# Last step of five feed-forwards: 512-column matmuls and sums of halves in place of three 256-column matmuls per block

## The chip, the core and the metric

The kernel runs on one core of one Trainium2 chip. The time is device time in microseconds of one execution. TensorE multiplies (its weight loads are listed apart, as PEld), VectorE (DVE), ScalarE (ACT) and GpSimd (POOL) do the rest, and SyncE (SP) issues the loads of the weights.

## The reference

Two transformer blocks over 256 tokens of width 1024, batch 1, in fp32. What matters here are its five feed-forward phases: a mixture of 32 experts of width 128, computed for all tokens and combined with routing weights, and four SwiGLU feed-forwards of width 2816 = 22 x 128.

```python
for e in range(N_EXPERTS):                                   # 32 experts
    hid = jax.nn.silu(xf @ w_gate[e]) * (xf @ w_up[e])
    y = y + combine[:, e:e + 1] * (hid @ w_down[e])

def swiglu(x, w_gate, w_up, w_down):                         # four times, D_FF = 2816
    return (jax.nn.silu(x @ w_gate) * (x @ w_up)) @ w_down
```

Between them stand a gated linear attention and a sparse attention (before the experts), a recurrent block (between `ffn0` and `ffn1`), keys and values (before `ffn2`) and an attention (before `ffn3`). Each of the four SwiGLU results is normalised (RMS) and added to the residual, half of it; the result of the experts is added directly.

## The kernel before

Every product is computed from operands split in two: `hi`, the value rounded to the matmul's fp32r format, and `lo`, the remainder. A product a*b is a_hi*b_hi + a_hi*b_lo + a_lo*b_hi, summed in PSUM; the helper `mm3` issues these three matmuls (lines 661 to 663).

Weights come in pieces of 128 x 1024 through a ring of six slots. SyncE loads a piece into `raw`, ScalarE rounds it to `w_hi` (line 1527, in loops line 1592), VectorE subtracts to get `w_lo` (line 2046, in loops 2051), and TensorE uses it. The order on each engine is written out by hand, and semaphores join them: `raw_in`, `hi_done`, `lo_done`, `used`.

A feed-forward of n steps (n = 32 for the experts, phase `moe`; n = 22 for `ffn0` to `ffn3`) handles 128 hidden channels per step f: the gate product, the up product, and the down product of step f - 1, one piece each. The hidden values are channel by token, 128 x 256. Two ways exist for a gate or up product of eight blocks of 128 inputs:

- `channel_major`, narrow: `mm3` for each block, 24 matmuls of 256 columns into one half of a PSUM bank.
- `channel_major_wide`: `both` holds the activations' `hi` and `lo` side by side, so one matmul of 512 columns gives w_hi*x_hi in the left half of the bank and w_hi*x_lo in the right one; w_lo*x_hi, 256 columns, is added to the left half. That is 8 matmuls of 512 and 8 of 256 columns (lines 747, 749, 750), and VectorE has to add the two halves (`tensor_reduce`, lines 2113 and 2153).

The steps inside a feed-forward are wide. The last step, n - 1, is narrow in the kernel before, in all five phases.

What VectorE does in a step: `scale_gate` multiplies the gate product by `rb`, the norm's factor per token (narrow: line 2110 straight from PSUM; wide: sum of halves, line 2113, then the multiply, line 2116). ScalarE applies SiLU (line 1587). `hidden` multiplies by `rb` again (line 2140), in `moe` by the combine weight (line 2145), then by the up product (narrow: line 2150; wide: sum of halves, line 2153, then line 2156), rounds it to `hid_hi` (line 2161) and takes the remainder `hid_lo` (line 2163), which releases TensorE's down product.

In the last step ScalarE splits the next phase's pieces behind SiLU, and `hidden` is given `beside`, the `w_lo` of the next piece, which VectorE does between line 2140 and the up product. `ffn3` is the last phase and has none. TensorE, behind its last up product, does the six matmuls of the down product of step n - 2 for the first token tile and first two column halves, waits for the last step's `hid_lo` (`hid_ready`), and then issues 18 more. The first finished quarter of the result goes to VectorE's residual sum (line 2257, in `moe`) or ScalarE's squares (line 1652).

Of the kernel before, what the change touches and what calls it, by code (L numbers as in the profile page):

```python
# [159 lines left out]
HID0 = {"moe": 0, "ffn0": E_N, "ffn1": E_N + FT, "ffn2": E_N + 2 * FT, "ffn3": E_N + 3 * FT}  # L160
# [8 lines left out]
def two_blocks(nc, A, consts, out):  # L169
    with ExitStack() as ctx:  # L170
# [78 lines left out]
        def sig(name):  # L249
            if name not in names:  # L250
                names[name] = sem(name)
            return names[name]
# [405 lines left out]
        def _(pe):  # L658
# [75 lines left out]
            def channel_major(s, o, step, xT=(xT_hi, xT_lo)):  # L734

                hi, lo = slot_view(w_hi, s, KT, P), slot_view(w_lo, s, KT, P)
                for k in range(KT):
                    m = mm3(o, hi[:, k, :], lo[:, k, :], xT[0][:, k, :], xT[1][:, k, :], k == 0, k == KT - 1)
                m.then_inc(used, step)
# [37 lines left out]
            def feed_forward(ph, n, begin, between, after_second=None, both=xT_both, norm_n=None):  # L777
                b = PLAN.start[ph]
                c0 = HID0[ph]
# [10 lines left out]
                def up_narrow(i, par, step):  # L790
                    s = (b + 3 * par) % RING
                    xT = (both[:, 0], both[:, 1])
                    pe.wait_ge(lo_done, i + 1)
                    channel_major(s, ps[:, 4 + par, 0:T], 1, xT)
                    pe.wait_ge(lo_done, i + 2)
                    channel_major((s + 1) % RING, ps[:, 6 + par, 0:T], step, xT)
# [8 lines left out]
                def down(hc, i, par, first, last, s=None):  # L805

                    if s is None:
                        s = (b + 3 * (1 - par) + 2) % RING
                    pe.wait_ge(hid_ready, hc)
                    pe.wait_ge(lo_done, i + 1)  # L810
                    for t in range(NT):
                        for h in range(2):
                            m = down_part(s, par, t, h, first, last)
                    m.then_inc(used, 1)
# [32 lines left out]
                f = n - 2  # L847
                up(None, f * 3 + b, 0)
                down(f + c0, f * 3 + b + 2, 1, False, False)
                up_narrow(f * 3 + b + 3, 1, 1)  # L850


                s0, s1 = (b + 3 * n - 1) % RING, (b + 3 * n) % RING
# [513 lines left out]
            b = PLAN.start["kv"]  # L1367
# [664 lines left out]
        def _(dve):  # L2032
# [7 lines left out]
            def lo(i, cols=PIECE, parts=P):  # L2040

                if i >= len(PLAN.real) or not PLAN.real[i]:
                    return
                dve.wait_ge(hi_done, i + 1)
                s = i % RING
                dve.tensor_tensor(w_lo[0:parts, s, 0:cols], raw[0:parts, s, 0:cols], w_hi[0:parts, s, 0:cols].bitcast(F32),  # L2046
                                  ALU.subtract).then_inc(lo_done, PLAN.step(i))

            def lo_at(s, w):
                dve.wait_ge(hi_done, w)  # L2050
                dve.tensor_tensor(w_lo[:, s, :], raw[:, s, :], w_hi[:, s, :].bitcast(F32), ALU.subtract)\  # L2051
                    .then_inc(lo_done, 1)
# [53 lines left out]
            def scale_gate(w_used, par, bank, both=None):  # L2106

                if both is None:
                    dve.wait_ge(used, w_used)
                    dve.tensor_tensor(sil[:, par, :], ps[:, bank, 0:T], rb[:], ALU.mult).then_inc(gate_scaled, 1)  # L2110
                    return
                dve.wait_ge(used, w_used)
                dve.tensor_reduce(sil[:, par, :], ps[:, bank, :].rearrange("p (a t) -> p t a", a=2), AX_X, ALU.add)\  # L2113
                    .then_inc(gate_sum, 1)
                dve.wait_ge(gate_sum, both)
                dve.tensor_tensor(sil[:, par, :], sil[:, par, :], rb[:], ALU.mult).then_inc(gate_scaled, 1)  # L2116

            def unweighted(f, w_used, bank):


                dve.wait_ge(silu_done, f + 1)
                dve.tensor_tensor(sil[:, f, :], sil[:, f, :], rb[:], ALU.mult).then_inc(hid_scl, 1)
                dve.wait_ge(hid_scl, f + 1)
                dve.wait_ge(used, w_used)
                dve.tensor_tensor(hid[:, f, :], sil[:, f, :], ps[:, bank, 0:T], ALU.mult).then_inc(hid_mul, 1)
# [40 lines left out]
            def feed_forward(ph, n, norm_n):  # L2166
                b, c0, moe = PLAN.start[ph], HID0[ph], ph == "moe"

                w0 = c0 - 2 * list(HID0).index(ph) - 3

                def step(f, pieces, beside=None):
                    for i in pieces[:2]:
                        lo(i)
                    if f == 0:
                        dve.wait_ge(norm_rb, RB_AT[norm_n])
                    banks = (4 + f % 2, 6 + f % 2)
                    wide = w0 + f if (3 if moe else 0) < f < n - 1 else None
                    scale_gate(b + 3 * f + 1, f % 2, banks[0], wide)
                    for i in pieces[2:]:
                        lo(i)  # L2180
                    c = c0 + f + 1
                    hidden(c, b + 3 * f + 2, f % 2, f if moe else None, c, f + 1, banks[1], beside, wide)

                if moe:
                    dve.wait_ge(norm_rb, RB_AT[1])
                    scale_gate(b + 1, 0, 0)
                    scale_gate(b + 4, 1, 5)
                    lo(b + 7)
                    unweighted(0, b + 3, 1)
                    unweighted(1, b + 5, 7)  # L2190
                    lo(b + 8)
                    lo(b + 9)
                    dve.wait_ge(sig("comb01_ok"), 1)
                    weighted(0)
                    weighted(1)
                    lo(b + 10)
                    scale_gate(b + 6, 0, 4)
                    lo(b + 11)
                    dve.wait_ge(sig("comb2_in"), 16)
                    hidden(3, b + 7, 0, 2, 3, 3, 6, free=b + 10)  # L2200
                    lo(b + 12)
                    scale_gate(b + 8, 1, 5)
                    lo(b + 13)
                    hidden(4, b + 9, 1, 3, 4, 4, 7, free=b + 11)
                    lo(b + 14)
                    dve.wait_ge(sig("comb_in"), 32)
                elif LEAD[ph] == 3:
                    lo(b + 4)
                    lo(b + 5)
                    dve.wait_ge(norm_rb, RB_AT[norm_n])  # L2210
                    scale_gate(b + 1, 0, 0)
                    lo(b + 6)
                    hidden(c0 + 1, b + 3, 0, None, c0 + 1, None, 1)
                    scale_gate(b + 4, 1, 5, w0 + 1)
                    lo(b + 7)
                    hidden(c0 + 2, b + 5, 1, None, c0 + 2, None, 7, both=w0 + 1)
                    lo(b + 8)
                    scale_gate(b + 6, 0, 4, w0 + 2)
                    lo(b + 9)
                    lo(b + 10)  # L2220
                    hidden(c0 + 3, b + 7, 0, None, c0 + 3, None, 6, both=w0 + 2, free=b + 8)
                    lo(b + 11)
                    scale_gate(b + 10, 1, 5, w0 + 3)
                    lo(b + 12)
                    hidden(c0 + 4, b + 11, 1, None, c0 + 4, None, 7, both=w0 + 3, free=b + 9)
                    lo(b + 13)
                    lo(b + 14)
                else:
                    step(0, [b + 3, b + 4, b + 5])
                    step(1, [b + 6, b + 7, b + 8])  # L2230
                with dve.Fori(4 if LEAD[ph] > 1 else 2, n - 2, 2) as f:
                    i0 = dve.snap(f * 3 + b)
                    for par in range(2):
                        for j in range(3):
                            off = 3 * par + 3 + j
                            lo_at((b + off) % RING, i0 + (off + 1))
                            if j == 1:
                                scale_gate(i0 + (3 * par + 1), par, 4 + par, dve.snap(f + (w0 + par)))
                        c = dve.snap(f + (c0 + par + 1))
                        e = dve.snap(f + par) if moe else None  # L2240
                        hidden(c, i0 + (3 * par + 2), par, e, c, c, 6 + par, None, dve.snap(f + (w0 + par)))
                step(n - 2, [b + 3 * n - 3, b + 3 * n - 2, b + 3 * n - 1])
                step(n - 1, [b + 3 * n], lambda: lo(b + 3 * n + 1))
                lo(b + 3 * n + 2)
# [492 lines left out]
            b = PLAN.start["kv"]  # L2737
# [34 lines left out]
            b = PLAN.start["q"]  # L2772
# [89 lines left out]
```

## Time and profile before

| | |
|---|---|
| median of three runs | 1543.87 us (1543.37 to 1545.18) |
| profiled execution | 1542.71 us, span 1540.8 us |
| TensorE busy (matmuls) | 1497.6 us, 97% |
| VectorE busy | 1201.1 us, 78% |
| ScalarE busy | 790.4 us, 51% |
| narrow multiplies of a gate product (line 2110) | 13, median 420 ns |
| sums of halves (lines 2113 and 2153) | 107 each, medians 691 and 692 ns |
| multiplies behind them (lines 2116 and 2156) | 107 each, median 425 ns |

The busy times of the engines overlap. A matmul's listed duration contains its way through the array, so matmuls that follow one another overlap: what one costs in a row of them is the distance from start to start. In a timeline the bracket behind a row tells how long the engine was idle before it and which instruction ended that.

### The profile page before, as it was taken

The numbers are of one execution on the slowest core, as the hardware profiler recorded it, in microseconds if no ns is written. First come the engines' busy times: TensorE is split into PE (matmuls) and PEld (weight loads), VectorE is DVE, ScalarE is ACT, GpSimd is POOL, SyncE is SP. The second block draws the span as 40 slices with busy tenths as digits, with TensorE's granted clock in tenths as the row PEclk, the third lists the DMA queues.
The fourth block names the chain that finished last, engine by engine and source line by source line (L and its number), as shares of the span: only waits on it lengthen the run. The fifth ranks groups of instructions, "written<-read, shape, count | busy, mean of one in ns | idle before, by whom it ended". The sixth has DMA issues, their size and how long they took to land.

```text
span 1540.8 us, 23595 instructions
## 1 busy us (share of the span) xinstructions
PE 1497.6 (97%) x8186; PEld 1282.1 (83%) x8186; DVE 1201.1 (78%) x2164; ACT 790.4 (51%) x1196; POOL 43.5 (3%) x68
## 2 busy tenths in 40 slices
PE   7989999999999999999999999999999999999998
PEld 6767789888888888887878888888888889888886
DVE  4876477988888888778688878785887786598886
ACT  6548554444444544446796434465444465554443
POOL 4100000000000300000000000000000000000000
PEclk9999999999999999999999999999999999999999
DMA  9635445755555676655244766644766643356661
GB/s 258 176 106 186 137 137 198 272 186 198 191 179 164 188 217 189 192 176 180 60 124 153 220 188 190 191 141 148 216 193 190 185 145 110 101 180 203 197 189 57
DMA packets 258540, 266.20 MB, mean 173 GB/s; under 512 B 10512, under 2 KB 210496, under 8 KB 258224
## 3 DMA queue, kind: packets, MB, share of 16 engines
q1 hardware_dynamic: 255040, 255.87, 54.7%
q0 software_dynamic: 3440, 9.54, 2.3%
q8 instruction: 36, 0.59, 0.2%
q14 instruction: 24, 0.20, 0.0%
HBM read 264.21 MB, written 1.09 MB: 172 GB/s over the span
## 4 chain that ended last, share of the span: by engine, by line
PE 85%; DVE 9%; ACT 4%; issue 2%; DMA 0%; DVEq 0%; SPq 0%; ACTq 0%
PE ps L747 22%; PE ps L661 13%; PE ps L749 13%; PE ps L663 13%; PE ps L662 13%; PE ps L750 3%; DVE w_lo L2046 2%; DVE xT_both L2090 1%; PE ps L1255 1%; ACT w_hi L1527 1%; PE ps L1416 1%; ACT sq L1652 0%; PE ps L691 0%; ACT xT_both L1536 0%; DVE arena L2333 0%
## 5 line engine op out<-in xcount | busy, mean ns | idle before, releaser
L1592 ACT ACTIVATE w_hi<-raw 128x1024 fp32r<-128x1024 f32 x276 | 290.8, 1058 | 159.3 <-PE ps L663 138.6
L2051 DVE TENSOR_TENSOR w_lo<-raw,w_hi 128x1024 fp32r<-128x1024 f32 x276 | 328.8, 1219 | 1.0
L747 PE MATMUL ps<-xT_both,w_hi 128*128 128x512 f32 x1218 | 306.6, 391 | 0.0
L2046 DVE TENSOR_TENSOR w_lo<-raw,w_hi 128x1024 fp32r<-128x1024 f32 (+4 forms) x209 | 247.1, 1210 | 42.3 <-ACT w_hi L1527 40.4
L747 PEld LDWEIGHTS ps<-xT_both,w_hi 128*128 128x128 f32 x1218 | 228.9, 188 | 45.9
L1587 ACT ACTIVATE hid_sil<-hid_sil 128x256 f32<-128x256 f32 x120 | 50.1, 418 | 360.1 <-DVE hid_sil L2116 318.9
L1527 ACT ACTIVATE w_hi<-raw 128x1024 fp32r<-128x1024 f32 (+4 forms) x209 | 210.9, 1048 | 29.6 <-PE ps L663 25.8
L749 PEld LDWEIGHTS ps<-xT_both,w_lo 128*128 128x128 f32 x1392 | 189.9, 190 | 13.6
L749 PE MATMUL ps<-xT_both,w_lo 128*128 128x256 f32 x1392 | 194.1, 282 | 0.0
L661 PE MATMUL ps<-w_hi,hid_hi 128*128 128x512 f32 x480 | 188.5, 393 | 0.8 <-DVE hid_lo L2163 0.7
L663 PE MATMUL ps<-w_hi,hid_lo 128*128 128x512 f32 x480 | 187.3, 390 | 0.0
L662 PE MATMUL ps<-w_lo,hid_hi 128*128 128x512 f32 x480 | 186.8, 389 | 0.0
L661 PE MATMUL ps<-w_hi,xT_both 128*128 128x512 f32 (+3 forms) x360 | 141.9, 394 | 13.7 <-DVE w_lo L2046 12.3
L2113 DVE TENSOR_REDUCE hid_sil<-ps 128x256 f32<-128x512 f32 x107 | 73.8, 690 | 98.9 <-PE ps L750 98.9
L663 PE MATMUL ps<-w_hi,xT_both 128*128 128x512 f32 (+3 forms) x360 | 137.8, 383 | 0.0
L662 PE MATMUL ps<-w_lo,xT_both 128*128 128x512 f32 (+3 forms) x360 | 137.7, 382 | 0.0
L663 PEld LDWEIGHTS ps<-w_hi,hid_lo 128*128 128x128 f32 x480 | 90.1, 188 | 20.0
L662 PEld LDWEIGHTS ps<-w_lo,hid_hi 128*128 128x128 f32 x480 | 90.2, 188 | 19.1
L661 PEld LDWEIGHTS ps<-w_hi,hid_hi 128*128 128x128 f32 x480 | 90.5, 188 | 17.8 <-DVE hid_lo L2163 3.3
L661 PEld LDWEIGHTS ps<-w_hi,xT_both 128*128 128x128 f32 (+1 forms) x360 | 68.7, 191 | 30.9 <-DVE w_lo L2046 9.2
L2153 DVE TENSOR_REDUCE hid_sil<-ps 128x256 f32<-128x512 f32 x107 | 74.0, 691 | 17.8 <-PE ps L750 15.1
L663 PEld LDWEIGHTS ps<-w_hi,xT_both 128*128 128x128 f32 (+1 forms) x360 | 68.5, 190 | 12.8
(395 smaller groups left out, 2160.0 us busy)
## 6 DMA issues: line engine op xcount, KB each, us to landing
raw<-in_ffn_w_gate_dram SPq DMA_DIRECT2D x88, 512.0 KB, 4.2
raw<-in_ffn_w_up_dram SPq DMA_DIRECT2D x88, 512.0 KB, 5.3
raw<-in_ffn_w_down_dram SPq DMA_DIRECT2D x88, 512.0 KB, 4.1
raw<-in_w_in_dram SPq DMA_DIRECT2D x40, 512.0 KB, 4.9
raw<-in_w_gate_dram SPq DMA_DIRECT2D x32, 512.0 KB, 3.5
raw<-in_w_up_dram SPq DMA_DIRECT2D x32, 512.0 KB, 4.3
raw<-in_w_down_dram SPq DMA_DIRECT2D x32, 512.0 KB, 3.5
raw<-in_rg_w_in_dram SPq DMA_DIRECT2D x16, 512.0 KB, 4.7
```

The lines of the kernel that those rows point to most:

```text
L661: pe.matmul(o, a_hi, b_hi, start=start, stop=False)
L662: pe.matmul(o, a_hi, b_lo, start=False, stop=False)
L663: return pe.matmul(o, a_lo, b_hi, start=False, stop=stop)
L747: pe.matmul(o, hi[:, k, :], both[:, :, k, :], start=k == 0, stop=False)
L749: pe.matmul(ps[:, bank, 0:T], lo[:, k, :], both[:, 0, k, :], start=False, stop=False)
L1527: act.activation(w_hi[0:parts, i % RING, 0:cols], raw[0:parts, i % RING, 0:cols], ACT.Copy)\
L1587: act.activation(sil[:, par, :], sil[:, par, :], ACT.Silu).then_inc(silu_done, 1)
L1592: act.activation(w_hi[:, s, :], raw[:, s, :], ACT.Copy).then_inc(hi_done, 1)
L2046: dve.tensor_tensor(w_lo[0:parts, s, 0:cols], raw[0:parts, s, 0:cols], w_hi[0:parts, s, 0:cols].bitcast(F32), ALU.subtract).then_inc(lo_do ...
L2051: dve.tensor_tensor(w_lo[:, s, :], raw[:, s, :], w_hi[:, s, :].bitcast(F32), ALU.subtract)\
L2113: dve.tensor_reduce(sil[:, par, :], ps[:, bank, :].rearrange("p (a t) -> p t a", a=2), AX_X, ALU.add)\
L2153: dve.tensor_reduce(hid[:, par, :], ps[:, bank, :].rearrange("p (a t) -> p t a", a=2), AX_X, ALU.add)\
```

## The change

TensorE's last step calls `up`, which is wide, in place of `up_narrow`. On VectorE the condition for `wide` includes the last step, and the count of sums done before a phase (`w0`) takes one less off per earlier phase, since each now has one step more with sums. Nothing else changes: the pieces, the loads, the order on ScalarE, GpSimd and SyncE are the same.

```diff
@@ TensorE, feed_forward
                 up(None, f * 3 + b, 0)
                 down(f + c0, f * 3 + b + 2, 1, False, False)
-                up_narrow(f * 3 + b + 3, 1, 1)
+                up(None, f * 3 + b + 3, 1)
@@ VectorE, feed_forward
-                w0 = c0 - 2 * list(HID0).index(ph) - 3
+                w0 = c0 - list(HID0).index(ph) - 3
...
                     banks = (4 + f % 2, 6 + f % 2)
-                    wide = w0 + f if (3 if moe else 0) < f < n - 1 else None
+                    wide = w0 + f if (3 if moe else 0) < f else None
                     scale_gate(b + 3 * f + 1, f % 2, banks[0], wide)
```

On TensorE, the start of the last step of `ffn0` stands like this before: behind the down product the three matmuls of `mm3` for the first block of the gate product, 256 columns each, which come eight times for the gate and eight times for the up product.

```order
L661 MATMUL ps<-w_hi,hid_hi 128x512
L662 MATMUL ps<-w_lo,hid_hi 128x512
L663 MATMUL ps<-w_hi,hid_lo 128x512
L661 MATMUL ps<-xT_both,w_hi 128x256
L662 MATMUL ps<-xT_both,w_hi 128x256
L663 MATMUL ps<-xT_both,w_lo 128x256
```

Now the same place, up to the next down product:

```order
L663 MATMUL ps<-w_hi,hid_lo 128x512
L747 MATMUL ps<-xT_both,w_hi 128x512 x7
L749 MATMUL ps<-xT_both,w_lo 128x256 x8
L750 MATMUL ps<-xT_both,w_hi 128x512
L747 MATMUL ps<-xT_both,w_hi 128x512 x7
L749 MATMUL ps<-xT_both,w_lo 128x256 x8
L750 MATMUL ps<-xT_both,w_hi 128x512
L661 MATMUL ps<-w_hi,hid_hi 128x512
```

48 matmuls have become 32, the first 16 for the gate and the last 16 for the up product; what stands ahead and behind is the same.

On VectorE, the last step of `ffn0` before, from the split of one piece to the remainder that TensorE waits for:

```order
L2046 TENSOR_TENSOR w_lo<-raw,w_hi 128x1024
L2110 TENSOR_TENSOR hid_sil<-ps,rb 128x256
L2140 TENSOR_TENSOR hid_sil<-hid_sil,rb 128x256
L2046 TENSOR_TENSOR w_lo<-raw,w_hi 128x1024
L2150 TENSOR_TENSOR hid_sil<-hid_sil,ps 128x256
L2161 CAST hid_hi<-hid_sil 128x256
L2163 TENSOR_TENSOR hid_lo<-hid_sil,hid_hi 128x256
```

And now:

```order
L2046 TENSOR_TENSOR w_lo<-raw,w_hi 128x1024
L2113 TENSOR_REDUCE hid_sil<-ps 128x256
L2116 TENSOR_TENSOR hid_sil<-hid_sil,rb 128x256
L2140 TENSOR_TENSOR hid_sil<-hid_sil,rb 128x256
L2046 TENSOR_TENSOR w_lo<-raw,w_hi 128x1024
L2153 TENSOR_REDUCE hid_sil<-ps 128x256
L2156 TENSOR_TENSOR hid_sil<-hid_sil 128x256
L2161 CAST hid_hi<-hid_sil 128x256
L2163 TENSOR_TENSOR hid_lo<-hid_sil,hid_hi 128x256
```

Each read of a product from PSUM has become a sum and a multiply; the split of a piece stands between the two products as before. The other four ends change alike, with the combine weight's multiply (line 2145) behind the split in `moe`, and without that split in `ffn3`.

## Rows read from the trace of the kernel before

**Rows 1.** The page: busy time by engine, and the last chain by engine.
```profile
PE 1497.6 (97%) x8186; PEld 1282.1 (83%) x8186; DVE 1201.1 (78%) x2164; ACT 790.4 (51%) x1196; POOL 43.5 (3%) x68
PE 85%; DVE 9%; ACT 4%; issue 2%; DMA 0%; DVEq 0%; SPq 0%; ACTq 0%
```

**Rows 2.** TensorE's waits: us in total, times, longest us.
```profile
PE ps L661 <- DVE hid_lo L2163: 0.7, 2, 0.5
```

**Rows 3.** Timeline, ffn3's step before the last: start us, us, engine, line, operation.
```profile
1513.20 1.75 PE L747 MATMUL ps<-xT_both,w_hi 128*128 128x512 f32 x7
...
1515.98 1.77 PE L747 MATMUL ps<-xT_both,w_hi 128*128 128x512 f32 x7
1516.18 0.69 DVE L2113 TENSOR_REDUCE hid_sil<-ps 128x256 f32<-128x512 f32 x1 [1.24 <-PE ps L750]
...
1517.36 0.42 ACT L1587 ACTIVATE hid_sil<-hid_sil 128x256 f32<-128x256 f32 x1 [2.84 <-DVE hid_sil L2116]
...
1518.77 0.40 PE L661 MATMUL ps<-w_hi,hid_hi 128*128 128x512 f32 x1
...
1519.04 0.69 DVE L2153 TENSOR_REDUCE hid_sil<-ps 128x256 f32<-128x512 f32 x1 [0.24 <-PE ps L750]
...
1520.22 0.29 DVE L2161 CAST hid_hi<-hid_sil 128x256 fp32r<-128x256 f32 x1
```

**Rows 4.** Timeline, ffn3's last step and what follows it.
```profile
1521.51 0.28 PE L661 MATMUL ps<-xT_both,w_hi 128*128 128x256 f32 x1
...
1524.58 0.42 DVE L2110 TENSOR_TENSOR hid_sil<-ps,rb 128x256 f32<-128x256 f32 x1 [2.47 <-PE ps L663]
...
1525.04 0.42 ACT L1587 ACTIVATE hid_sil<-hid_sil 128x256 f32<-128x256 f32 x1 [6.31 <-DVE hid_sil L2110]
...
1527.26 0.40 PE L661 MATMUL ps<-w_hi,hid_hi 128*128 128x512 f32 x1
...
1527.53 0.42 DVE L2150 TENSOR_TENSOR hid_sil<-hid_sil,ps 128x256 f32<-128x256 f32 x1 [1.61 <-PE ps L663]
...
1527.99 0.29 DVE L2161 CAST hid_hi<-hid_sil 128x256 fp32r<-128x256 f32 x1
...
1528.80 0.50 PE L661 MATMUL ps<-w_hi,hid_hi 128*128 128x512 f32 x1
...
1529.80 0.60 ACT L1652 ACTIVATE sq<-ps 128x512 f32<-128x512 f32 x1 [2.82 <-PE ps L663]
```

**Rows 5.** Timeline, the end of ffn1's last step.
```profile
1006.39 0.42 DVE L2110 TENSOR_TENSOR hid_sil<-ps,rb 128x256 f32<-128x256 f32 x1 [2.47 <-PE ps L663]
...
1007.17 2.94 ACT L1527 ACTIVATE w_hi<-raw 128x1024 fp32r<-128x1024 f32 x3
...
1008.25 1.22 DVE L2046 TENSOR_TENSOR w_lo<-raw,w_hi 128x1024 fp32r<-128x1024 f32 x1 [0.52 <-ACT w_hi L1527]
...
1009.39 0.41 DVE L2150 TENSOR_TENSOR hid_sil<-hid_sil,ps 128x256 f32<-128x256 f32 x1
...
1010.23 0.39 PE L663 MATMUL ps<-w_hi,hid_lo 128*128 128x512 f32 x1
...
1010.65 0.50 PE L661 MATMUL ps<-w_hi,hid_hi 128*128 128x512 f32 x1
...
1011.64 0.60 ACT L1652 ACTIVATE sq<-ps 128x512 f32<-128x512 f32 x1
```

**Rows 6.** Timeline, the end of the last step of moe.
```profile
498.87 0.42 DVE L2145 TENSOR_TENSOR hid_sil<-hid_sil,arena 128x256 f32<-128x256 f32 x1
...
500.59 0.50 PE L661 MATMUL ps<-w_hi,hid_hi 128*128 128x512 f32 x1 [0.49 <-DVE hid_lo L2163]
```

**Rows 7.** Stretches: us, busy by engine, PEclk (granted clock), DMA share, GB/s.
```profile
60.41:66.30 5.89, 3.41 (x15) 2.89 (x16) 5.79 (x9) 4.44 (x5) 0.00 (x0) 1.00 0.41 126
98.30:102.46 4.16, 0.00 (x0) 0.00 (x0) 4.09 (x6) 3.31 (x4) 0.00 (x0) 0.99 0.01 2
102.46:105.93 3.47, 3.47 (x9) 2.76 (x9) 3.44 (x3) 0.00 (x0) 0.00 (x0) 0.52 0.67 195
```

## The prediction

> **What bounds the kernel now.** I read the page's shares first: TensorE is busy 97% of the span, VectorE 78%, and the chain that ended last is TensorE for 85% and VectorE for 9% [rows 1]. So what counts is TensorE's own time and the few places where it waits. The waits view has only one entry in which TensorE waits for the hidden values of a feed-forward: 0.7 us in 2 waits [rows 2]. Read alone, this says that the last step's work on VectorE is nearly hidden. Whether it is hidden with room to spare only the timeline tells, so next I read the end of three feed-forwards.
>
> A wide step is seen in [rows 3] (step 20 of `ffn3`), the narrow last step behind it in [rows 4], the end of `ffn1` in [rows 5], which stands for `ffn0`, `ffn1` and `ffn2` (three ends with the same distances within 0.02 us), the end of `moe` in [rows 6]. In [rows 5] the six matmuls that cover the wait end at 1010.23 + 0.39 = 1010.62, and the next matmul, which needs `hid_lo`, starts at 1010.65. TensorE stands still for 0.03 us: the two engines arrive together. In `moe` it already waits, 0.49 us [rows 6]. There is no slack under VectorE's chain at any of these ends. The chain from the first half of the last step is: gate sum on VectorE, SiLU on ScalarE, scaling by `rb`, then the split of the next piece (`w_lo`), then the up product, the rounding, the remainder, and TensorE goes on.
>
> **TensorE's part.** The narrow step has 2 x 24 matmuls of 256 columns, the wide one 2 x (8 of 512 and 8 of 256): the same 12,288 columns, in 32 instructions in place of 48. The wide pair takes 1518.77 - 1513.20 = 5.57 us [rows 3], the narrow pair 1527.26 - 1521.51 = 5.75 us [rows 4]. Gain 0.18 us in each of five feed-forwards, 0.90 us in all if nothing waited. One wide half takes 2.78 (1513.20 to 1515.98).
>
> A rule speaks of this. By the Trainium skill, "TensorE: Matmul & The Clock Gate", section "Back-to-back issue gap", matmuls follow each other by their columns at 2.4 GHz and a fixed 2.5 ns. By it the narrow pair would take 5.24 us and the wide 5.20, an estimate, so the gain would be 0.04 us; the lead of 0.09 us that the sum below uses would be 0.02, four times, and the 0.18 of the last end 0.04, which makes the loss 0.42 us larger. The trace does not agree in this size (0.18), and I take the trace.
>
> **VectorE, first half (gate).** Narrow: one multiply, and SiLU starts 1525.04 - 1524.58 = 0.46 us after it [rows 4]. Wide: the sum of the halves, then the multiply, and SiLU starts 1517.36 - 1516.18 = 1.18 us after [rows 3]: +0.72. Against it the first half is ready earlier: the wide sum starts 1516.18 - 1513.20 = 2.98 us after the first matmul of the step, the narrow multiply 1524.58 - 1521.51 = 3.07. SiLU is therefore late by 0.72 - 0.09 = **0.63 us**.
>
> What is queued behind it: ScalarE splits the next pieces behind SiLU (`w_hi`, 1007.17), and VectorE's `w_lo` starts only when the first has come (1008.25, idle 0.52 until then) [rows 5]. So `w_lo` moves by the same 0.63 us, and the up product stands directly behind it at 1009.39, with no idle time. In `moe` the multiplication with the combine weights stands between (498.87) [rows 6]; it moves too.
>
> **VectorE, second half (up).** Narrow: product to rounding 1527.99 - 1527.53 = 0.46 us [rows 4]. Wide: sum, then product, to rounding 1520.22 - 1519.04 = 1.18 us [rows 3]: **+0.72 us**. It can't slip under anything, since VectorE runs in order and was held by `w_lo` until then. Nor does it wait for TensorE: in [rows 5] the wide pair would be ready about 1009.15 (1006.39 - 3.07 + 2.78 + (1519.04 - 1515.98)), and VectorE comes to it at 1009.39 + 0.63 = 1010.02.
>
> **Sum at `moe`, `ffn0`, `ffn1`, `ffn2`:** 0.63 + 0.72 = 1.35 us later, and the 0.18 us of TensorE turns into more waiting. TensorE's idle time goes from 0.49 to 0.49 + 0.18 + 1.35 = 2.02 us in `moe` and from 0.03 to 1.56 us in the other three. Four times 1.35 is 5.40 us.
>
> **Sum at `ffn3`.** It is the last phase and has no piece to split, so VectorE waits for TensorE before the up product (1.61 us idle, [rows 4]) and the late gate is covered by that idle time. TensorE brings the second half 0.18 us earlier, the sum of halves costs 0.72: **+0.54 us**.
>
> **What follows.** After TensorE resumes the same 18 matmuls run. The first ScalarE pass over the result starts 1011.64 - 1010.65 = 0.99 us after the resumption in `ffn1` [rows 5] and 1529.80 - 1528.80 = 1.00 us in `ffn3` [rows 4], where ScalarE is idle before it. So although in `ffn1` ScalarE comes to it straight from its table load, TensorE's result is just as late there; ScalarE is moved by 0.63 us only, TensorE by 1.35, and the whole 1.35 passes on. The later norm, its transposes and the next phase descend from this result.
>
> Total: 5.40 + 0.54 = 5.94 us. Nothing is added that the trace lacks; unknown is only what a longer stop of TensorE does (clock, below) and whether a later stage absorbs it. The lower bound is the loss wholly hidden or given back and the 0.90 us of TensorE kept, -0.9 us; the upper is four clock drops, +12.6 us. I take 5.94, since every link of it is a distance in the rows and the ends meet without slack. The profiled execution took 1542.71 us (span 1540.8 and 1.9 around it); with the change it would be 1548.65. The median of the runs is 1543.87, 1.16 us above that execution; with 5.94 it is 1549.81, **forecast 1549.8 us**, 0.38% slower.
>
> **Rivals.**
>
> *The next phase gives it back (not slower).* Place: the first pair of pieces behind each of the first four feed-forwards. If there the wait that ends last were one for pieces whose load or split is not moved, the 1.35 us would vanish in it; the 0.54 us of `ffn3`, behind which nothing comes, would stay, so +0.5 us, 1544.4 us. It decides where this phase stood for more than 1.35 us on something independent. For it: loads and ScalarE's splits move by 0.63 us at most. Against it: the chain is TensorE and VectorE for 94% and rows for a DMA are 0% [rows 1], and the residual and the norm can't start without the result. Were the gain of TensorE to come out as well, it would be 1543.0 us; for that the sums of halves would have to be covered, and the 0.03 us in [rows 5] leaves no cover. Chance 0.10, of which 0.01 for this last form.
>
> *TensorE's clock falls in the longer stops.* The trace shows a stretch with a stop of 5.89 - 3.41 = 2.48 us in which the granted clock stayed 1.00, that is 2.4 GHz, and one of 4.16 us after which it was 0.52 for 3.47 us, nearly all of it at 1.2 GHz [rows 7]. That costs 3.47 x 0.48 = 1.67 us each. Four times: +6.7 on top, 1556.5 us; only behind `moe`, whose stop is the longest: 1551.5 us. The stops I expect, 2.02 and 1.56 us, are shorter than the one that did no harm. The Trainium skill ("TensorE: Matmul & The Clock Gate", section "What's actually happening") says that the default is the slow clock and that activity releases it; the trace agrees, with 0.52 behind the long stop. Chance 0.05 for one or more.
>
> *Only one of the two terms is paid.* If the split of the next piece did not wait on ScalarE's order behind SiLU, the gate's delay would be hidden as in `ffn3`: 4 x 0.72 + 0.54 = 3.4 us, 1547.3 us. The 0.52 us of idle time before `w_lo`, released by ScalarE [rows 5], speaks against it. Chance 0.06.
>
> *The change doesn't do what it says* (the last step stays narrow somewhere): the order of the changed program shows all five ends wide on both engines. Chance nil.
>
> **How the numbers follow.** Forecast 0.79, given back 0.10, one term 0.06, clock 0.05. Its own range is 1548.3 to 1551.3: the terms are good to some 0.3 us together, the medians to about 1 us. For 8 in 10 with the neighbouring cases in part I take 1546.8 to 1552.5. A measurement of this kernel tells 0.2%, 3.1 us, from no change. Slower by more: the forecast, the clock and half of the one-term case, 0.87. Within: 0.12. Faster: 0.01, as even the pure gain of 0.90 us lies within.
>
> **What would show it.** In the changed profile: the waits view has TensorE waiting for `hid_lo` at all five ends, some 2.0, 1.6, 1.6, 1.6 and 0.7 us; SiLU at 1.18 us behind the gate's sum; `w_lo` moved with it; from the first matmul of the last step to the resumption 7.29 us in `ffn3` are now 7.83; granted clock 1.00 there. TensorE's busy time falls by some 0.9 us. If the stops are there but the span grows by less than 4 us, the giving back is right and the place is the next phase. If the resumption moves by 0.7 us only, the ScalarE link is wrong.

## The result and the profile after

The changed kernel took 1551.38 us (median of 5, 1549.63 to 1552.30) beside 1543.87 us for the kernel before (median of 5, 1542.76 to 1545.18): ratio 1.0047, 95% interval 1.0033 to 1.0062. It is slower by 7.5 us where 5.94 were forecast, within the range of 1546.8 to 1552.5 and 0.1 us above the narrower one that the prediction gives its own mechanism. Timed again it took 1550.27 beside 1544.43 us, ratio 1.0040 (1.0026 to 1.0054), 5.8 us. The profiled execution took 1549.63 us, with a span of 1547.8 us beside 1540.8.

The page of the changed kernel, busy time and last chain, answering to [rows 1]:

```profile
PE 1497.4 (97%) x8106; PEld 1277.7 (83%) x8106; DVE 1208.2 (78%) x2174; ACT 790.4 (51%) x1196; POOL 43.5 (3%) x68
PE 84%; DVE 10%; ACT 3%; issue 2%; DMA 0%; DVEq 0%; SPq 0%; ACTq 0%
```

There are 80 matmuls less, yet TensorE's busy time is 0.2 us less, not 0.9. The five ends alone have 0.87 us less; 0.53 us more than before stands ahead of the last step of `moe`, in code that the change does not touch, where the two executions also have their low clock in different places. VectorE has ten instructions and 7 us more. The page hardly shows the loss; TensorE's waits do (us in total, times, longest), answering to [rows 2]:

```profile
PE ps L661 <- DVE hid_lo L2163: 7.7, 6, 2.0
```

From 0.7 to 7.7 us, of which the five ends have 7.5. The end of `ffn3` in the timeline, answering to [rows 3, 4]:

```profile
1528.01 1.75 PE L747 MATMUL ps<-xT_both,w_hi 128*128 128x512 f32 x7
...
1530.98 0.69 DVE L2113 TENSOR_REDUCE hid_sil<-ps 128x256 f32<-128x512 f32 x1 [2.37 <-PE ps L750]
...
1532.16 0.42 ACT L1587 ACTIVATE hid_sil<-hid_sil 128x256 f32<-128x256 f32 x1 [6.94 <-DVE hid_sil L2116]
...
1533.57 0.40 PE L661 MATMUL ps<-w_hi,hid_hi 128*128 128x512 f32 x1
...
1533.84 0.69 DVE L2153 TENSOR_REDUCE hid_sil<-ps 128x256 f32<-128x512 f32 x1 [0.80 <-PE ps L750]
...
1535.03 0.29 DVE L2161 CAST hid_hi<-hid_sil 128x256 fp32r<-128x256 f32 x1
...
1535.83 0.50 PE L661 MATMUL ps<-w_hi,hid_hi 128*128 128x512 f32 x1 [0.72 <-DVE hid_lo L2163]
...
1536.83 0.60 ACT L1652 ACTIVATE sq<-ps 128x512 f32<-128x512 f32 x1 [2.74 <-PE ps L663]
```

TensorE's pair takes 1533.57 - 1528.01 = 5.56 us, the gate's sum starts 2.97 us after the first matmul, SiLU 1.18 after that, the rounding 1.19 after the second sum, and the resumption comes after 7.82 us (7.29 before). VectorE still waits 0.80 us for TensorE before the second sum (1.61 before): here the gate's delay is covered. The end of `ffn1`, answering to [rows 5]:

```profile
1006.99 1.75 PE L747 MATMUL ps<-xT_both,w_hi 128*128 128x512 f32 x7
...
1009.96 0.69 DVE L2113 TENSOR_REDUCE hid_sil<-ps 128x256 f32<-128x512 f32 x1 [2.37 <-PE ps L750]
...
1011.48 2.94 ACT L1527 ACTIVATE w_hi<-raw 128x1024 fp32r<-128x1024 f32 x3
...
1012.55 1.23 DVE L2046 TENSOR_TENSOR w_lo<-raw,w_hi 128x1024 fp32r<-128x1024 f32 x1 [0.52 <-ACT w_hi L1527]
...
1013.69 0.68 DVE L2153 TENSOR_REDUCE hid_sil<-ps 128x256 f32<-128x512 f32 x1
...
1015.68 0.50 PE L661 MATMUL ps<-w_hi,hid_hi 128*128 128x512 f32 x1 [1.58 <-DVE hid_lo L2163]
...
1016.67 0.60 ACT L1652 ACTIVATE sq<-ps 128x512 f32<-128x512 f32 x1 [0.75 <-PE ps L663]
```

`w_lo` starts 2.59 us behind the gate's first VectorE instruction (1.86 before), still with 0.52 us of waiting for ScalarE, and the second sum has no idle time ahead of it. TensorE stands still for 1.58 us where it stood for 0.03. The squares still start 0.99 us behind the resumption, and ScalarE now waits 0.75 us for them. The end of `moe`, answering to [rows 6]:

```profile
500.41 0.42 DVE L2145 TENSOR_TENSOR hid_sil<-hid_sil,arena 128x256 f32<-128x256 f32 x1
...
502.86 0.50 PE L661 MATMUL ps<-w_hi,hid_hi 128*128 128x512 f32 x1 [2.03 <-DVE hid_lo L2163]
```

The length of an end, from the last step's first matmul to the resumption, is the measure for all that follows. In the profiled executions:

| end | moe | ffn0 | ffn1 | ffn2 | ffn3 | sum of differences |
|---|---|---|---|---|---|---|
| before | 7.80 | 7.33 | 7.33 | 7.31 | 7.29 | |
| changed | 9.15 | 8.69 | 8.69 | 8.71 | 7.82 | +6.00 us |

Forecast was 5.94. The span grew by 7.0 us; nearly all of the rest, 0.92 us, is already there when the last step of `moe` begins (493.71 beside 492.79). Stretches of the changed kernel, columns as in [rows 7]:

```profile
62.48:65.90 3.42, 3.42 (x9) 2.73 (x10) 3.42 (x4) 1.82 (x2) 0.00 (x0) 0.55 0.78 230
502.86:506.30 3.44, 3.44 (x15) 2.87 (x16) 2.77 (x4) 0.00 (x0) 0.00 (x0) 1.00 0.64 174
```

The first stands behind the same early stop (2.43 us here) as the first of [rows 7]. There the granted clock stayed 1.00; here it is 0.55, mostly 1.2 GHz. This is code that the change does not touch. In the profiles of the other kernels below the beginning of that step lies 0.4 us earlier to 2.4 us later than before, and 0.4 earlier in one that has both products wide: the shift belongs to the execution, not to the change. Behind the new stop of `moe` the clock stayed 1.00 in this execution.

### The profile page after: what moved, and what is told of

Same layout as the page of the kernel before. It is cut to its first block, busy times and chain, and to the rows that moved or that the text cites. A ratio compares the mean times of both kernels' runs of the same rounds, so it can differ in the third digit from the quotient of the medians.

```text
span 1547.8 us, 23445 instructions
## 1 busy us (share of the span) xinstructions
PE 1497.4 (97%) x8106; PEld 1277.7 (83%) x8106; DVE 1208.2 (78%) x2174; ACT 790.4 (51%) x1196; POOL 43.5 (3%) x68
## 4 chain that ended last, share of the span: by engine, by line
PE 84%; DVE 10%; ACT 3%; issue 2%; DMA 0%; DVEq 0%; SPq 0%; ACTq 0%
PE ps L747 23%; PE ps L749 14%; PE ps L661 13%; PE ps L663 12%; PE ps L662 12%; PE ps L750 3%; DVE w_lo L2046 2%; DVE xT_both L2090 2%; PE ps L1255 1%; ACT w_hi L1527 1%; PE ps L1416 1%; PE ps L691 0%; ACT sq L1652 0%; ACT xT_both L1536 0%; DVE arena L2333 0%
## 5 line engine op out<-in xcount | busy, mean ns | idle before, releaser
L747 PE MATMUL ps<-xT_both,w_hi 128*128 128x512 f32 x1274 | 320.6, 391 | 0.0
L747 PEld LDWEIGHTS ps<-xT_both,w_hi 128*128 128x128 f32 x1274 | 239.4, 188 | 48.0
L749 PEld LDWEIGHTS ps<-xT_both,w_lo 128*128 128x128 f32 x1456 | 198.6, 190 | 14.2
L749 PE MATMUL ps<-xT_both,w_lo 128*128 128x256 f32 x1456 | 203.0, 282 | 0.0
L2113 DVE TENSOR_REDUCE hid_sil<-ps 128x256 f32<-128x512 f32 x112 | 77.3, 690 | 109.7 <-PE ps L750 109.6
L2153 DVE TENSOR_REDUCE hid_sil<-ps 128x256 f32<-128x512 f32 x112 | 77.4, 691 | 18.9 <-PE ps L750 16.2
```

Of the source, the lines that this page charges most:

```text
L747: pe.matmul(o, hi[:, k, :], both[:, :, k, :], start=k == 0, stop=False)
L749: pe.matmul(ps[:, bank, 0:T], lo[:, k, :], both[:, 0, k, :], start=False, stop=False)
L2153: dve.tensor_reduce(hid[:, par, :], ps[:, bank, :].rearrange("p (a t) -> p t a", a=2), AX_X, ALU.add)\
```

## The experiments

**The changed kernel again**, without an edit.

> The changed kernel unaltered, timed again. In its first profile the five ends add up to the 5.9 us of the forecast, but the span grew by 7.0 us; about 0.9 us of it was there before the last step of moe began. Theory (the first 0.9 us is spread between executions, not the change): the five ends again add 5.9 us in the profile (1.35 each at moe, ffn0, ffn1, ffn2 and 0.54 at ffn3), the shift at the beginning of the last step of moe is another number than 0.9, anywhere within 1 us of zero, and the median is 5 to 7 us over the kernel before. Rival (the longer program or its other layout costs 0.9 us or more ahead of the first changed instruction): that shift is 0.9 us again and the median is 7.5 us over.

1550.27 us (1549.86 to 1553.07), +5.8. The profile is that of the execution with 1553.07 us, span 1551.3. Its ends are 9.14, 8.69, 8.69, 8.71 and 7.83 us, +6.00 again. But the shift at the beginning of moe's last step was 1.57, not within 1 us of zero, and a new loss is seen behind the stop of `moe`. TensorE's timeline there (start us, us), and two stretches:

```profile
503.50 0.50 PE L661 MATMUL ps<-w_hi,hid_hi 128*128 128x512 f32 x1 [2.04 <-DVE hid_lo L2163]
...
504.71 0.63 PE L662 MATMUL ps<-w_lo,hid_hi 128*128 128x512 f32 x1
505.14 0.63 PE L663 MATMUL ps<-w_hi,hid_lo 128*128 128x512 f32 x1
...
509.34 2.17 PE L691 MATMUL ps<-con,x_res 128*128 128x128 f32 x16
...
513.25 0.39 PE L769 MATMUL ps<-xT_both,w_hi 128*128 128x256 f32 x1 [1.74 <-ACT xT_both L1536]
```

```profile
504.30:507.70 3.40, 3.40 (x9) 2.63 (x8) 1.61 (x3) 0.00 (x0) 0.00 (x0) 0.50 0.64 196
514.50:517.90 3.40, 3.40 (x18) 3.40 (x18) 3.20 (x12) 3.33 (x8) 3.10 (x6) 0.51 0.19 44
```

0.80 us behind the resumption the clock falls to 0.50 for 3.4 us, and matmuls follow each other by 0.43 us instead of 0.23. From the resumption to the transposes it takes 5.84 us, where the profile before it had 4.21: 1.6 us lost. A second fall stands in the norm behind `moe`, where TensorE waits 1.74 us (1.73 in the kernel before); together they cost 2.9 us by the starts of ffn0's last step, 1.2 of it in the norm. So the clock rival of the prediction is real at `moe`, in some executions. The fall in the norm is another matter: the wait there is as long without the change. Of the twelve profiles here, of all kernels, in which nothing fills it, seven have a fall, among them the two with one product wide and the one with the split moved, whose clock stayed behind the stop of `moe`.

**VectorE's part alone, and TensorE's part alone.** Both take one half of the change:

```diff
 VectorE's part alone: the changed kernel with
-                up(None, f * 3 + b + 3, 1)
+                up_narrow(f * 3 + b + 3, 1, 1)
 TensorE's part alone: the kernel before with
-                up_narrow(f * 3 + b + 3, 1, 1)
+                up(None, f * 3 + b + 3, 1)
```

> VectorE's part alone: TensorE's last step stays narrow (48 matmuls), VectorE sums both halves of the bank in it. The right half then holds what the step before left there, so the last step's values are not those of the reference; the work is that of the change. Theory (VectorE's and ScalarE's chain sets every end): SiLU comes 0.72 us later behind the gate product, the up part takes 0.72 us more; from the first matmul of the last step to the resumption 7.33 becomes 8.77 us in ffn0, ffn1 and ffn2, 7.80 becomes 9.24 in moe, 7.29 becomes 8.01 in ffn3: 4 x 1.44 + 0.72 = +6.5 us over the kernel before, 0.5 us more than the whole change. Rival (TensorE hides part of it): less than +5 us. Rival (wide matmuls are what costs): about zero here.

> TensorE's part alone: its last step is wide (32 matmuls), VectorE reads only the left half of the bank in it, so w_hi times the activations' remainder is left out of the last step. Theory: the gate product is ready 0.09 us earlier and the chain behind it moves by that, -0.09 us at moe, ffn0, ffn1 and ffn2; at ffn3, where TensorE comes last, -0.18 us: -0.5 us in all, less than can be timed. TensorE waits 0.09 us more at the first four ends. Rival (the 0.18 us comes out everywhere): -0.9 us and no longer waits. Rival (something in the wide step itself is slow): a positive difference.

Neither computes the last step's values in full: the first adds to each product what a wide step had left in the right half of the bank (the same bank is used by every second step), the second leaves out w_hi times the activations' remainder.

VectorE's part: 1551.89 us, ratio 1.0046 (1.0032 to 1.0060); ends 9.25, 8.79, 8.78, 8.77, 8.02: +6.56, expected 6.5. TensorE's part: 1543.61 us, ratio 0.9996 (0.9987 to 1.0005), no difference that the timing tells; ends 7.68, 7.23, 7.23, 7.26, 7.11: -0.55, expected -0.5. Its wait in `moe` is 0.58 us (0.49 before), as expected 0.09 more. All of the loss is VectorE's, and TensorE's 0.18 us comes out whole only at `ffn3`.

**One product wide, the other narrow.** In the last step only; an excerpt, for the gate wide. With the up product wide the two conditions change places, and the calls in the other steps take the counts that go with them:

```diff
-                up(None, f * 3 + b + 3, 1)
+                wide_narrow(f * 3 + b + 3, 1)    # or narrow_wide: channel_major_wide for one, channel_major for the other
-                    wide = w0 + f if (3 if moe else 0) < f else None
+                    wide_g = w0 + f if (3 if moe else 0) < f else None            # gate wide
+                    wide_u = w1 + f if (3 if moe else 0) < f < n - 1 else None    # up narrow
```

> In the last step only the gate product is wide (its sum of halves on VectorE), the up product narrow. Theory (ScalarE's order behind SiLU carries the gate's delay to w_lo and so to the up product): 0.63 us later at moe, ffn0, ffn1 and ffn2, and at ffn3, where VectorE has idle time before the up product, the delay is covered and TensorE's earlier end gives -0.09 us: +2.4 us in all. From the first matmul of the last step to the resumption 7.33 becomes 7.96 us in ffn1. Rival (only the up half is paid, the gate is hidden everywhere): 7.33 becomes 7.24 or stays, 0 us in all.

> In the last step only the up product is wide, the gate narrow. Theory: +0.72 us at moe, ffn0, ffn1 and ffn2, and 0.72 - 0.09 = +0.63 at ffn3: +3.5 us in all; from the first matmul of the last step to the resumption 7.33 becomes 8.05 us in ffn1. With the run of the wide gate alone this adds up to the whole change, 2.4 + 3.5 = 5.9. Rival (the two halves cover each other): the sum of the two runs differs from the whole change's by more than 0.5 us in the profiled distances.

Gate wide: 1546.24 beside 1543.88 us, ratio 1.0014 (1.0004 to 1.0024); ends 8.42, 7.96, 7.95, 7.99, 7.19, +2.45. Up wide: 1547.21 us, ratio 1.0022 (1.0013 to 1.0032); ends 8.52, 8.06, 8.06, 8.04, 7.93, +3.55. The two add up to 6.00, the whole change. Both terms of the prediction stand, and so does the cover of the gate at `ffn3`.

**`w_lo` behind `hid_lo`.** The split of the next piece leaves the chain:

```diff
-                step(n - 1, [b + 3 * n], lambda: lo(b + 3 * n + 1))
+                step(n - 1, [b + 3 * n])
+                lo(b + 3 * n + 1)
```

> The changed kernel with the split of the next piece on VectorE (w_lo) moved behind the remainder hid_lo in the last step. Theory (the gate's delay costs only because w_lo waits for ScalarE and stands ahead of the up product): all ends look like ffn3's, TensorE brings the up product last: from the first matmul of the last step to the resumption 7.83 us in ffn0 to ffn3 and the same in moe, where the kernel before had 7.80. So at the resumption +0.03 us in moe and about +0.5 at the other four. Behind it VectorE now has one split more (1.14 us) with only 0.71 us of idle time, so up to 0.4 us is lost there per end: +2 to +4 us over the kernel before, 2 to 4 us less than the whole change. Rival (the loss is in the sums alone, wherever w_lo stands): no gain against the whole change.

> Gate product wide, up product narrow, w_lo behind hid_lo: the one form in which TensorE's gain of the gate half is kept and the sum of halves is covered by the wait for the up product. Theory: from the first matmul of the last step to the resumption 7.29 - 0.09 = 7.20 us at all five ends, against 7.80, 7.33 (three) and 7.29 before: -0.6 in moe and -0.1 at each of the others, -1.0 us in all before what the moved split costs behind it (up to 0.4 us at three ends, and the residual sum of moe starts later, but its last part is set by TensorE). Between -1 and +0.5 us: no difference that can be timed, the profile has to show it. Rival (the split behind hid_lo delays the norm in full, 1.14 us at each): +3.5 us.

With both products wide: 1545.97 us, ratio 1.0013 (1.0003 to 1.0022), 4.3 and 5.4 us less than the changed kernel in its two timings. All five ends are alike: 7.82, 7.83, 7.83, 7.87, 7.83, in sum 3.9 us less than in the changed kernel. TensorE's waits for `hid_lo` (us in total, times, longest):

```profile
PE ps L661 <- DVE hid_lo L2163: 3.9, 6, 0.7
```

Five stops of 0.72 to 0.74 us in place of 2.03, three of 1.58, and 0.72: the gate's sum costs nothing once `w_lo` does not carry it to the up product. The 3.9 us are more than the gate's 2.45, since the split's own time has left the chain too. The kernel before with the split moved was not run, so what the move alone is worth is not shown. It cost less behind the ends than the 0.4 us per norm that I allowed: TensorE waits 0.58 us for the first `x_res` tile in `ffn1`, 0.50 before.

With the gate wide and the up product narrow the ends are the shortest of all, 7.19, 7.18, 7.19, 7.15, 7.19: -1.16 us. The time is 1544.72 beside 1543.88, ratio 1.0009 (0.9999 to 1.0018), no gain. VectorE behind the end of `ffn1`:

```profile
1010.30 0.42 DVE L2157 TENSOR_TENSOR hid_sil<-hid_sil,ps 128x256 f32<-128x256 f32 x1 [0.89 <-PE ps L663]
...
1011.43 2.35 DVE L2053 TENSOR_TENSOR w_lo<-raw,w_hi 128x1024 fp32r<-128x1024 f32 x2
1013.99 0.69 DVE L2279 TENSOR_TENSOR xn<-ps,g_post 128x512 f32<-128x512 f32 x1 [0.21 <-ACT sq L1659]
```

and TensorE's wait behind it:

```profile
1017.95 1.16 PE L691 MATMUL ps<-con,x_res 128*128 128x128 f32 x8 [1.14 <-DVE x_res L2297]
```

The end is 0.14 us shorter, but VectorE has two splits (2.35 us) ahead of the norm, ScalarE three and its table load behind a later SiLU, and TensorE then waits 1.14 us for `x_res` where it waited 0.50. Of the expectation (-1.0, up to 0.4 back at three ends) the first part came and the second was too small: 0.65 to 0.70 us went back at each of three. Only `moe` (-0.61) and `ffn3` (-0.10) keep their gain; a kernel with that form in these two alone would save 0.7 us, an estimate from these two ends, below what the timing tells, and was not run.

**More sums.** The up product's sum done again, with the same result:

```diff
                     dve.wait_ge(used, w_used)
+                    for _ in range(more):      # 1, or 4, in the last step
+                        link(dve.tensor_reduce(hid[:, par, :], ps[:, bank, :].rearrange("p (a t) -> p t a", a=2), AX_X, ALU.add))
```

> The changed kernel with the sum of halves of the up product done twice in the last step (same result). Theory (nothing covers VectorE's chain, 1 us there is 1 us of time): 0.72 us more at each of five ends, +3.6 us over the changed kernel; TensorE's waits become 2.75 us in moe, 2.3 at three ends and 1.44 in ffn3; the granted clock stays 1.00 behind them. Rival (a part is covered downstream): less than +2.5 us in the distances from end to end.

> The changed kernel with the sum of halves of the up product done five times in the last step (same result). Theory: 2.9 us more at each of five ends, +14.4 us over the changed kernel from the chain alone. TensorE now stops for 4.9 us in moe, 4.5 at three ends and 3.6 in ffn3, as long as the one stop of 4.16 us in the kernel before behind which its granted clock was 0.52; if the clock falls behind these too, each costs up to 1.7 us more: +14.4 to +22.8 us, I expect it at moe and at least one more, about +18. Rival (the clock rival of the prediction would also be right at 2 us): a lower clock already shows in the run with one more sum.

One more: 1556.99 beside 1543.83 us, ratio 1.0077 (1.0060 to 1.0094), 13.2 us. The ends are 9.87, 9.41, 9.41, 9.44, 8.55: +3.62 over the changed kernel, the term as expected. But the clock did not stay 1.00. TensorE's resumption in `moe` and the stretch around it:

```profile
503.66 0.79 PE L661 MATMUL ps<-w_hi,hid_hi 128*128 128x512 f32 x1 [2.76 <-DVE hid_lo L2166]
```

```profile
503.30:507.00 3.70, 3.34 (x8) 2.67 (x9) 2.50 (x4) 0.00 (x0) 0.00 (x0) 0.54 0.47 128
```

In this execution it fell at all of the first four ends, whose stops are 2.76 and three of 2.30 us, and in the norm behind `moe`. Behind `moe` a fall cost 1.5 us again, but from the resumption to the next end's last step the distances of `ffn0`, `ffn1` and `ffn2` grew by 0.8, 0.5 and 0.5 us only: at `ffn0` 1.6 us were lost up to the beginning of the norm, and half of it came back in the norm, where TensorE's wait of 0.5 us for `x_res` is gone. The four executions have mean clocks of 0.990 to 0.995 and times of 1553.1 to 1558.3 us. Four more: 1571.13 us, ratio 1.0172 (1.0155 to 1.0189), 27.3 us over before, of which the ends have 20.5. The stops of 4.9, 4.5 (three) and 3.6 us all had a fall of the clock with them, for 6.8 us at each but `moe`; at `ffn0`:

```profile
699.67:706.50 6.83, 6.83 (x18) 5.34 (x19) 4.68 (x11) 2.95 (x9) 0.00 (x0) 0.55 0.27 77
```

So 1 us on VectorE's chain is 1 us of time, and above it the clock adds more with a longer stop: from the resumption of `ffn0` to the last step of `ffn1` 2.1 us here, 0.8 with one more sum. The rival is right in this: the lower clock shows with one more sum, and in one of two profiles with none.

**The stops filled.** Matmuls that nobody reads, before the wait for the last `hid_lo`, and for two runs also in the norm behind `moe`, the only one ahead of a feed-forward that has none:

```diff
+                keep_warm({"moe": 14, "ffn3": 4}.get(ph, 10), 4)    # last run: moe 4, ffn3 1, others 3
                 pe.wait_ge(hid_ready, c0 + n)
-            WARM = {..., 2: (0, 0, 0), ...}
+            WARM = {..., 2: (0, 0, 12), ...}                        # last run: (0, 0, 3)
```

> The changed kernel, and TensorE's stop before hid_lo filled with matmuls whose result nobody reads (14 of 256 columns in moe, 10 in ffn0 to ffn2, 4 in ffn3, into a bank that is free). They end before hid_lo comes, so the ends keep their lengths (9.15, 8.69, 8.69, 8.70, 7.82 us from the last step's first matmul to the resumption). In one of two profiles of the changed kernel the granted clock fell to 1.2 GHz for 3.4 us right behind the stop of moe, in the other not. Theory (the part of the time above the forecast comes from such falls in some executions): no fall behind any of the five stops; the fall in the norm behind moe stays possible; median 5.4 to 6.6 us over the kernel before. Rival (the excess is elsewhere): 7 us or more.

> As the run with the filled stop, and twelve matmuls whose result nobody reads in the 1.74 us that TensorE waits in the norm behind moe, the one norm that has none in the kernel before. Theory: no fall of the granted clock between the first 120 us and the end in any execution; mean clock 0.996 or 0.997 in each; median 5 to 6 us over the kernel before (which has such a fall itself in some executions), 0.3 to 1 us below the run with the filled stop alone, and a narrower spread. Rival (the fall in the norm does not depend on that wait): clock and spread as with the filled stop alone.

Both missed, by my own arithmetic: 1561.67 us (ratio 1.0115, 1.0098 to 1.0132) and 1564.11 us (1.0131, 1.0114 to 1.0148). I had counted 0.12 us for each of them, the distance of the fp32r matmuls. They are fp32, and each is two matmuls in the trace; 14 of them take 5.85 us, not 1.7, and the end of `moe` becomes 12.80 us:

```profile
500.69 6.20 PE L671 MATMUL ps<-con 128*128 128x256 f32 x28
506.54 0.58 PE L661 MATMUL ps<-w_hi,hid_hi 128*128 128x512 f32 x1
```

Their times say nothing on the excess. In both profiles the clock did not fall behind any end or in that norm.

> The filled stops again, at the right size. In the two runs before, each call of 256 columns was two matmuls in the trace and took 0.44 us, so that the filling outlasted the stop by 3.7 us in moe. Now 4 calls in moe (1.8 us of the 2.03), 3 in ffn0 to ffn2 (1.3 of 1.57), 1 in ffn3 (0.4 of 0.72), 3 in the norm behind moe (1.3 of 1.74). Theory (what the changed kernel loses above 5.9 us is the granted clock's fall behind the stop of moe and in the norm behind it, in some executions): the ends keep 9.15, 8.69, 8.69, 8.70 and 7.82 us, the granted clock does not fall between 120 us and the end, and the five executions have no mean clock below 0.995; median 1549.0 to 1550.2 us, +5 to +6 over a before of about 1544. Rival (the excess is no matter of the clock): 1551 us or more, as in the first timing, with the ends unchanged.

1549.04 us (six executions, 1548.10 to 1549.32) beside 1543.81 us, ratio 1.0033 (1.0021 to 1.0045): +5.2 us. The ends are unchanged, 9.14, 8.68, 8.69, 8.71, 7.82. The end of `moe` and the 20 us around it:

```profile
499.81 1.89 PE L671 MATMUL ps<-con 128*128 128x256 f32 x8
502.01 0.50 PE L661 MATMUL ps<-w_hi,hid_hi 128*128 128x512 f32 x1 [0.31 <-DVE hid_lo L2164]
```

```profile
500.00:520.00 20.00, 19.26 (x119) 16.70 (x119) 15.69 (x41) 13.38 (x32) 12.37 (x13) 1.00 0.53 146
```

All six executions have a mean clock of 0.996 or 0.997. The ten executions of the unfilled changed kernel have 0.994 to 0.996 and reach from 1549.63 to 1553.07 us; the three of them with 0.996 took 1549.63, 1549.86 and 1550.27. The rival (1551 us or more) is out: with the stops and the norm filled, which changes no end, no execution is as long as the shortest of those ten. The run does not tell the two apart: a kernel with only the stops filled to measure was not run, and the wait in the norm stays unfilled in the kernel before. That 5.2 us is less than the 6.0 of the ends may come from executions of the kernel before that carry the norm's 1.2 us, where these do not; the interval (3.2 to 6.9 us) holds both, and it is not shown.

## Why the prediction was right, and where it was not

- *VectorE and ScalarE set the ends, without slack.* Right. The waits are 2.03, three of 1.57 or 1.58, and 0.72 us, where 2.02, 1.56 and 0.7 were forecast.
- *Gate +0.63, carried by ScalarE's order to `w_lo`.* Right: +0.62 to +0.68 with the gate alone wide, -0.10 at `ffn3`, and gone when `w_lo` stands behind.
- *Up +0.72.* Right: +0.72 or +0.73 at four ends, +0.64 at `ffn3`, as the terms say.
- *TensorE's gain of 0.18 us per pair.* Right: half of it, the gate's 0.09, moves the chain and is in the 0.63; the rest only lengthens four of the five stops. The 0.04 us that follows from the Trainium skill's formula ("TensorE: Matmul & The Clock Gate", section "Back-to-back issue gap") did not come: the part alone brought 0.18 at `ffn3`. That section gives the formula for a matmul by itself and says that a stream with weight loads goes by other distances, which the prediction passed over; the distances here are 0.12 us at 256 columns and 0.23 at 512.
- *All of it passes on.* Right: between the ends nothing is given back. The next end's start moves by the same amount, within 0.05 us, wherever the clock is alike.
- *The clock stays.* Wrong as a certainty: I reasoned from one stop of 2.48 us behind which the clock stayed and gave a fall 0.05. The same early stop had a fall in the changed kernel's first profile, and a stop of 2.04 us in the second. One quiet execution said too little. The rival's price of 1.67 us per fall was about right behind `moe` (1.6) and too high at `ffn0` to `ffn2` (0.8 and 0.5 with one more sum), and the norm behind `moe` was missing from it.
- *The size.* The sum of the ends is 6.0 us in both profiles of the changed kernel; the two timings gave 7.5 and 5.8, and both intervals (5.1 to 9.6 and 4.0 to 8.3 us) hold the forecast of 5.94. So the 1.5 us of the first timing above the ends are not clear of noise. Falls of the clock are what the profiles show that can make them, but how often the clock falls in the kernel before, where the early stop and the norm are the same, stays open: its executions also reach down to a mean clock of 0.994, and none of those was profiled.

## What to carry to other kernels

At the end of a loop count the chain that the last matmul releases, not the matmuls: there the sum that a wider matmul leaves to VectorE is paid in full, while inside the loop the next step's products cover it. Look then at what stands in order between the halves of such a chain; here moving one split of the next phase's weights out of it took back 3.9 of the 6.0 us. And one execution's granted clock is one draw: behind a new TensorE stop of 2 us one of two executions of the same program lost another 1.6 us.

## What the hardware showed that was not expected

- With stops of nearly the same length the granted clock fell in one execution and not in another. The early stop of 2.4 to 2.5 us, the same code in every kernel, had a fall in 7 of the 14 profiles (2.43 us in the changed kernel's first; none at 2.42 us in the last run's). The wait of 1.73 or 1.74 us in the norm behind `moe` had one in 7 of 12, and a fall there cost 1.2 us. At the end of `moe`: 2.03 us no, 2.04 us yes.
- A fall lasted 3.4 us, with four more sums also 6.8. In the second profile of the changed kernel it came 0.8 us after the resumption; with one more sum the fall at `moe` began 0.2 us before it, while TensorE still stood, and those at the other three ends 0.9 to 1.4 us after.
- Filling matmuls need not fill all: with 0.31 us left empty of 2.03, and 0.44 of 1.74 in the norm, the six executions agree within 0.1%, against 0.2% for the changed kernel.
- A matmul of 256 columns on fp32 operands is two in the trace and takes 0.43 us where it follows its like, that on fp32r operands 0.12 us.
